# Softmax rows in step: three rows' TensorE work at one place between weight pieces

## The chip, the cores and the metric

The kernel runs on one core of a Trainium2 chip. The metric is the device time of one execution in microseconds. Five engines work side by side, each through its own queue in program order, and they are held together by semaphores: TensorE (PE in the profile, with PEld for its weight loads), VectorE (DVE), ScalarE (ACT), GpSimd (POOL) and SyncE (SP), which issues most of the DMAs.

## The reference, cut to what matters

One layer of a hybrid encoder runs on 1024 prompt frames and 64 sample frames (1088 columns in all). Of it the attention branch and the gate multiply matter here:

```
proj = rmsnorm(x) @ w_in                      # 2048 -> u, z_ssm, q, k, v, z_att, f
q, k = rmsnorm(q per head), rmsnorm(k per head)
logit[t, s] = q_t . k_s / sqrt(128) + (c_t - c_s),  s <= t
o = softmax(logit) @ v                        # 8 heads of 128
y_att = rmsnorm(o * silu(z_att)); y_ssm = ... zs * sigmoid(zs @ w_glu + b)
out = x + concat(y_ssm, y_att) @ w_out
```

A prompt row block i (128 queries) sees keys 0 to 128(i+1). The sample block (64 queries) sees 128 cached keys and its own 64.

## The kernel before, in words

The state-space stage comes first, then the attention stage, then the output projection. The attention stage is nine passes of one function, `part(h, gemm, att, ha)`, which every engine has in its own form. Pass 0 makes q, k, v and z of head 0. Passes 1 to 7 make those of head h and, between the weight matmuls, run the softmax attention of head h-1. Pass 8 (gemm False) runs the w_glu multiply with the attention of head 7 between. Every pass has 32 slots s. In each slot TensorE first multiplies one weight piece (18 matmuls, L192), and whatever the tables name for this slot follows behind it: a "place". Nine row blocks are handled in the order ROWS (0, 1, 2, 8, 3, 4, 5, 6, 7), 8 being the sample block. S_AT names the slots of the logits (L1997, L2001), T_AT those of the transposes of the probabilities (L2018, L2021), and O_AT those of the product with v (L1976, L1978).

The engines beside TensorE walk the same 32 slots in program order. In slot s ScalarE casts the high part of the weight piece s+4 (L176), which it may do once piece s is multiplied, and VectorE subtracts the low part (L180). TensorE therefore has its pieces split some three ahead. Then, if the tables say so:

- S: VectorE reduces the logits from PSUM (L1795, L1797, L1800), ScalarE takes the exponential (L1592), VectorE waits for it and multiplies by the reciprocal of the sum (L1804, L1805). The probabilities have one buffer, PR.
- T: ScalarE (L1602) and, beyond 512 columns, VectorE (L1809) copy the transposes from TB to PT.
- O: VectorE multiplies the result into ZR (L1782).
- SQ_AT (slots 8 and 19): ScalarE and VectorE square q or k (L1614, L1819, L1822: SQH, SQ and SQL). SS_AT (slots 9 and 20): TensorE sums the squares over the partitions, SQH first (L1959), then SQL (L1962), into TB.
- RT_AT, REC_AT: ScalarE takes the root; VectorE takes the reciprocals in eight pieces (L1829), for q in slots 11 to 18, for k in slots 22, 22, 23, 23, 25, 25, 26, 26. In slot 18 VectorE scales q (L1836), in slot 27 k (L1838). The squares of k wait for the scaling of q, since both use SQ.
- At slots 7, 15 and 23, where a group of eight pieces ends, ScalarE copies two thirds of the finished q, k or v out of the banks GB (L1551, L1553) and VectorE one third (L1760), as the first thing in the slot. The first piece of the next group may write bank 1 only when VectorE's copy is done. In pass 8 a group has four pieces, and ScalarE's tanh (L1544) empties all three banks at slots 3, 7, 11 and so on.

Of the kernel before, what the change touches and what calls it, by code (L numbers as in the profile page):

```python
# [21 lines left out]
D_MODEL, SEQ, DEC, PAST = 2048, 1024, 64, 128  # L22
# [5 lines left out]
P = 128  # L28
# [24 lines left out]
def build_kernel(nc, x_prompt, x_sample, cache_k, cache_v, cache_logf, state_ssm_re, state_ssm_im,  # L53
# [17 lines left out]
    def stand(eng, name):  # L71

        eng.sem_inc(sem("stand_" + name), 1)
# [46 lines left out]
    with ctx:  # L120
        sb = pool_of(ctx)
        ident = sb("ident", [P, P])
# [1037 lines left out]
        def attention(st, W, past):  # L1160
# [33 lines left out]
            NR = 9  # L1194
# [79 lines left out]


            ROWS = (0, 1, 2, 8, 3, 4, 5, 6, 7)
            S_AT = (0, 3, 5, 7, 10, 13, 16, 21, 24)
            T_AT = (2, 4, 6, 8, 12, 15, 18, 23, 26)
            O_AT = (3, 5, 7, 9, 13, 16, 19, 24, 27)
            KPT_AT = 5  # L1280
            SQ_AT = {8: (0, QR), 19: (1, KR)}
            SS_AT = {9: (0, 4), 20: (1, 7)}
            RT_AT = {9: 0, 20: 1}
            REC = 8
            REC_AT = ((11, 12, 13, 14, 15, 16, 17, 18), (22, 22, 23, 23, 25, 25, 26, 26))
# [7 lines left out]
            def keys(i):  # L1293

                return (P * (i + 1), P) if i < NR - 1 else (PAST + DEC, DEC)

            def row_at(s, at):

                return ROWS[at.index(s)], at.index(s)
# [185 lines left out]
            def scalar(act, tail):  # L1485
# [40 lines left out]
                def part(h, gemm, att, ha):  # L1526
                    last = isinstance(h, int) and h == NH - 1
                    for s in range(NPC):
# [51 lines left out]
                        if gemm and s in RT_AT:  # L1580
# [4 lines left out]
                            S.activation(SQ[:, SEQ:TOK], TB[:, 3 * 512:3 * 512 + DEC], ACT.Sqrt, bias=epsc[:],  # L1585
                                         scale=1.0 / HD).then_inc(e["rt"], 1)
                            table(ACT.Exp)
                        if att and s in S_AT:
                            i, p = row_at(s, S_AT)
                            w, n = keys(i)  # L1590
                            act.wait_ge(e["nmx"], NR * ha + p + 1)
                            S.activation(PR[0:n, 0:w], PR[0:n, 0:w], ACT.Exp, bias=nmx[0:n],  # L1592
                                         accum_out=rsum[0:n]).then_inc(e["exp"], 1)
                        if att and s == KPT_AT:
                            act.wait_ge(e["kpt_mm"], ha + 1)
                            S.copy(KPT[:], TB[:, 1024:1024 + PAST]).then_inc(e["kpt"], 1)
                        if att and s in T_AT:
                            i, p = row_at(s, T_AT)
                            act.wait_ge(e["pt_mm"], NR * ha + p + 1)
                            if i < NR - 1:  # L1600
                                b = min(i + 1, 4) * P
                                S.copy(PT[:, 0:b], TB[:, 1024:1024 + b]).then_inc(e["pt_act"], 1)  # L1602
                            else:
                                S.copy(PT[:, 0:DEC], TB[:, 1024:1024 + DEC])
                                S.copy(PT[0:DEC, P:P + DEC], TB[0:DEC, 1024 + P:1024 + P + DEC]).then_inc(e["pt_act"], 1)
                        if gemm and s in SQ_AT:
                            w, raw = SQ_AT[s]
                            act.wait_ge(e["ga"], 9 * h + 2 * w + 2)
                            act.wait_ge(e["gd"], 3 * h + w + 1)
                            if w:  # L1610
                                act.wait_ge(e["ss_mm"], 2 * h + 1)
                            elif att:
                                act.wait_ge(e["v_mm"], h)
                            S.activation(SQH[:], raw[:], ACT.Square).then_inc(e["sq"], 1)  # L1614
# [65 lines left out]
            def vector(dve, tail):  # L1680
# [66 lines left out]
                def part(h, gemm, att, ha):  # L1747
                    last = isinstance(h, int) and h == NH - 1
                    for s in range(NPC):
# [27 lines left out]
                        if att and s in O_AT:  # L1777

                            i, p = row_at(s, O_AT)
                            n = keys(i)[1]  # L1780
                            dve.wait_ge(e["o_mm"], NR * ha + p + 1)
                            V.tensor_tensor(ZR[:, i * P:i * P + n], TB[:, 4 * 512:4 * 512 + n], ZR[:, i * P:i * P + n],  # L1782
                                            ALU.mult).then_inc(e["y"], 1)
                        if att and s in S_AT:
                            i, p = row_at(s, S_AT)
                            w, n = keys(i)
                            c = 0 if i < NR - 1 else SEQ
                            if p == 0:
                                dve.wait_ge(e["in"], 48 * (ha + 1))
                            o.then(V.tensor_tensor(DM[0:n, 0:n], NCB[0:n, c + w - n:c + w], maskb[0:n, 0:n], ALU.add))  # L1790
                            dve.wait_ge(e["s_mm"], NR * ha + p + 1)
                            stand(dve, "dve")

                            if w > n:
                                V.tensor_tensor_reduce(out=PR[0:n, 0:w - n], in0=TB[0:n, 0:w - n], in1=NCB[0:n, c:c + w - n], scale=1.0,  # L1795
                                                       scalar=-3e38, op0=ALU.add, op1=ALU.max, accum_out=mx[0:n])
                            o.then(V.tensor_tensor_reduce(out=PR[0:n, w - n:w], in0=TB[0:n, w - n:w], in1=DM[0:n, 0:n], scale=1.0,  # L1797
                                                          scalar=-3e38, op0=ALU.add, op1=ALU.max, accum_out=md[0:n]))
                            if w > n:
                                V.tensor_scalar(nmx[0:n], md[0:n], mx[0:n], -1.0, ALU.max, ALU.mult).then_inc(e["nmx"], 1)  # L1800
                            else:
                                V.tensor_scalar(nmx[0:n], md[0:n], -1.0, None, ALU.mult).then_inc(e["nmx"], 1)
                            dve.wait_ge(e["exp"], NR * ha + p + 1)
                            o.then(V.reciprocal(rrec[0:n], rsum[0:n]))  # L1804
                            V.tensor_scalar(PR[0:n, 0:w], PR[0:n, 0:w], rrec[0:n], None, ALU.mult).then_inc(e["pn"], 1)  # L1805
                        if att and s in T_AT and 4 <= row_at(s, T_AT)[0] < NR - 1:
                            i, p = row_at(s, T_AT)
                            dve.wait_ge(e["pt_mm"], NR * ha + p + 1)
                            V.tensor_copy(PT[:, 512:P * (i + 1)], TB[:, 1536:1024 + P * (i + 1)]).then_inc(e["pt_dve"], 1)  # L1809
                        if gemm and s in SQ_AT:  # L1810
                            w, raw = SQ_AT[s]
                            dve.wait_ge(e["ga"], 9 * h + 2 * w + 2)
# [94 lines left out]
            def tensor(pe, tail):  # L1907
                def part(h, gemm, att, ha):
                    for s in range(NPC):
# [34 lines left out]
                        if gemm and s in SS_AT:  # L1944
# [3 lines left out]
                            pe.wait_ge(e["sq"], 2 * h + w + 1)  # L1948
                            if att:
                                pe.wait_ge(e["nmx"], NR * ha + p)  # L1950
                            if not att and w == 0:
                                pe.wait_ge(past["z_act"], 8)
                                pe.wait_ge(past["fin_ev"], 8)
                            elif not att:
                                pe.wait_ge(e["g_cum"], 2)
                                pe.wait_ge(e["g_ev"], 2)
# [7 lines left out]
                        if att and s in O_AT:  # L1964
# [12 lines left out]
                            else:  # L1977
                                T.matmul(O, CV[:], PT[:, 0:DEC], start=True, stop=False)  # L1978
                                ins = T.matmul(O, VT[0:DEC, TT - 1], PT[0:DEC, P:P + DEC], start=False, stop=True)
                            ins.then_inc(e["o_mm"], 1)  # L1980
                        if att and s in S_AT:
                            i, p = row_at(s, S_AT)
                            w, n = keys(i)
# [17 lines left out]
                                T.matmul(TB[0:DEC, 0:PAST], q, KPT[:], start=True, stop=True)  # L2001
                                ins = T.matmul(TB[0:DEC, PAST:w], q, KN[:, SEQ:TOK], start=True, stop=True)
                            ins.then_inc(e["s_mm"], 1)
                        if att and s == KPT_AT:
                            pe.wait_ge(e["in"], 48 * (ha + 1))
                            pe.wait_ge(e["pt_act"], NR * ha + sum(t < s for t in T_AT))
                            T.transpose(TB[:, 1024:1024 + PAST], CK[:], ident[:]).then_inc(e["kpt_mm"], 1)
                        if att and s in T_AT:
                            i, p = row_at(s, T_AT)
                            w, n = keys(i)  # L2010
                            pe.wait_ge(e["pn"], NR * ha + p + 1)
                            if s > KPT_AT:
                                pe.wait_ge(e["kpt"], ha + 1)
                            if p:
                                pe.wait_ge(e["pt_act"], NR * ha + p)
                            if i < NR - 1:
                                for b in range(i + 1):
                                    ins = T.transpose(TB[:, 1024 + b * P:1024 + (b + 1) * P], PR[:, b * P:(b + 1) * P], ident[:])  # L2018
                            else:
                                stand(pe, "pe")  # L2020
                                T.transpose(TB[:, 1024:1024 + DEC], PR[0:DEC, 0:PAST], ident[0:DEC, 0:DEC])  # L2021
                                ins = T.transpose(TB[0:DEC, 1024 + P:1024 + P + DEC], PR[0:DEC, PAST:w], ident[0:DEC, 0:DEC])
                            ins.then_inc(e["pt_mm"], 1)
                        if gemm and s in (KT_AT, VT_AT):
                            src, base, name = (KN, 0, "k") if s == KT_AT else (VR, 1024, "v")
                            if s == KT_AT:
# [152 lines left out]
```

## Time and profile before

| | us |
|---|---|
| median of 3 runs | 1982.18 (1981.3 to 1983.46) |
| the profiled execution | 1982.17, of which the span is 1980.6 |
| TensorE busy | 1940.0 (98%) |
| VectorE busy | 985.9 (50%) |
| ScalarE busy | 646.7 (33%) |
| GpSimd busy | 405.8 (20%) |

The mean granted clock of TensorE is 0.994 of full speed. A row of the timeline gives the start and the duration of one instruction or of a few alike. Matmuls overlap each other in the pipeline, so durations of TensorE don't add up: lengths are read there from start to start.

### The profile page before, as it was taken

What the parts mean: (1) busy time and instruction counts of PE and PEld (TensorE: products, weight loads), DVE (VectorE), ACT (ScalarE), POOL (GpSimd) and SP (SyncE); (2) the same over time, 40 slices, a digit from 0 to 9 for tenths busy, and PEclk for the clock granted to TensorE, in tenths of its full rate; (3) what the DMA queues carried; (4) which work ended last, traced back from release to release, by engine and by line L of the source; (5) the groups of instructions that cost most, each with busy time, mean ns of one, the idle gap of its engine ahead of it and who ended that gap; (6) DMA issues with size and microseconds to landing.
All of it is one profiled execution on the core that took longest, in us unless ns stands there. A gap on an engine that the chain in (4) does not pass through costs nothing.

```text
span 1980.6 us, 32524 instructions
## 1 busy us (share of the span) xinstructions
PE 1940.0 (98%) x11552; PEld 1810.3 (91%) x11552; DVE 985.9 (50%) x1899; ACT 646.7 (33%) x1274; POOL 405.8 (20%) x706
## 2 busy tenths in 40 slices
PE   5999999999999999999999999999999999999999
PEld 4899999999989999999999999999998988888887
DVE  7865566555454553645446355463565652222221
ACT  6432233332342333333433343334354441111110
POOL 5865444555210010010100101001010021010100
PEclk8999999999999999999999999999999999999999
DMA  8344343344322112121211212112165452222221
GB/s 227 105 116 103 108 111 99 107 120 122 97 55 66 36 49 70 32 86 34 72 45 34 83 34 83 37 36 82 32 234 178 139 201 91 93 94 90 96 91 46
DMA packets 194132, 180.06 MB, mean 91 GB/s; under 512 B 32179, under 2 KB 165389, under 8 KB 192853
## 3 DMA queue, kind: packets, MB, share of 16 engines
q1 hardware_dynamic: 176832, 127.97, 23.5%
q0 software_dynamic: 11712, 40.12, 6.0%
q10 hardware_dynamic: 5524, 11.14, 1.6%
q8 instruction: 38, 0.62, 0.1%
q14 instruction: 26, 0.21, 0.0%
HBM read 133.24 MB, written 45.93 MB: 90 GB/s over the span
## 4 chain that ended last, share of the span: by engine, by line
PE 90%; DVE 5%; issue 2%; DMA 1%; POOL 1%; ACT 1%; SPq 0%; DVEq 0%; POOLq 0%; ACTq 0%
PE GB L192 56%; PE TB L2087 4%; PE TB L2088 4%; PE TB L2089 4%; PE TB L1976 3%; PE TB L1997 3%; PE GB L2087 2%; PE GB L2088 2%; PE GB L2089 2%; PE TB L2018 2%; PE TB L1144 1%; PE TB L1145 1%; PE GB L1055 1%; PE TB L1134 1%; PE TB L2037 1%
## 5 line engine op out<-in xcount | busy, mean ns | idle before, releaser
L192 PE MATMUL GB<-XH,whi 128*128 128x384 f32 x2448 | 829.3, 339 | 6.0 <-DVE UP L749 5.5
L192 PE MATMUL GB<-XH,wlo 128*128 128x384 f32 x2448 | 801.5, 327 | 0.0
L192 PE MATMUL GB<-XL,whi 128*128 128x384 f32 x2448 | 798.9, 326 | 0.0
L192 PEld LDWEIGHTS GB<-XH,whi 128*128 128x128 f32 x2448 | 460.4, 188 | 21.4 <-issue 8.3
L192 PEld LDWEIGHTS GB<-XL,whi 128*128 128x128 f32 x2448 | 460.7, 188 | 5.3 <-issue 3.8
L192 PEld LDWEIGHTS GB<-XH,wlo 128*128 128x128 f32 x2448 | 459.9, 188 | 0.0
L180 DVE TENSOR_TENSOR wlo<-wraw,whi 128x256 fp32r<-128x256 f32 x412 | 206.1, 503 | 506.1 <-ACT whi L176 502.0
L176 ACT CAST whi<-wraw 128x256 fp32r<-128x256 f32 x412 | 166.4, 406 | 627.3 <-PE GB L192 618.4
L1409 POOL DMA_DIRECT2D ya_s<-ZR x7 | 4.1, 584 | 729.6 <-DVE ZR L1782 729.6
L1829 DVE RECIPROCAL SQ<-SQ 128x136 f32<-128x136 f32 x128 | 127.5, 996 | 1.1
L1592 ACT ACTIVATE PR<-PR,nmx 128x128 f32<-128x128 f32 (+8 forms) x72 | 53.4, 742 | 183.2 <-DVE nmx L1800 171.1
L2087 PE MATMUL TB<-OHI,XH 128*128 128x512 f32 x240 | 93.8, 391 | 0.0
L2088 PE MATMUL TB<-OHI,XL 128*128 128x512 f32 x240 | 93.6, 390 | 0.0
L2089 PE MATMUL TB<-OLO,XH 128*128 128x512 f32 x240 | 93.4, 389 | 0.0
L1722 DVE TENSOR_TENSOR OLO<-OLF,OHI 128x512 fp32r<-128x512 f32 x48 | 33.3, 700 | 100.6 <-ACT OHI L1524 100.6
L1882 DVE SCALAR_TENSOR_TENSOR XO<-TB,CK,XO 128x512 f32<-128x512 f32 x40 | 28.1, 747 | 109.9 <-PE TB L2089 109.9
L1976 PE MATMUL TB<-PT,VT 128*128 128x128 f32 x576 | 74.6, 275 | 0.0
L1997 PE MATMUL TB<-KN,QN 128*128 128x512 f32 (+2 forms) x192 | 72.5, 486 | 0.0
L1976 PEld LDWEIGHTS TB<-PT,VT 128*128 128x128 f32 x576 | 71.4, 191 | 0.3 <-DVE PT L1809 0.3
L1524 ACT CAST OHI<-OLF 128x512 fp32r<-128x512 f32 x48 | 29.5, 620 | 110.3 <-DMA OLF<-in_w_out 110.2
L1490 ACT ACT_TABLE_LOAD x48 | 61.6, 1283 | 0.8
L1795 DVE CUSTOM_DVE_ANT_0 PR<-TB,NCB 128x128 f32<-128x128 f32 (+3 forms) x64 | 40.9, 640 | 34.8 <-PE TB L1997 24.0
(426 smaller groups left out, 2606.3 us busy)
## 6 DMA issues: line engine op xcount, KB each, us to landing
wraw<-in_w_in SPq DMA_DIRECT2D x380, 128.0 KB, 2.2
OLF<-in_w_out SPq DMA_DIRECT2D x48, 256.0 KB, 3.0
XO<-in_x_prompt POOLq DMA_DIRECT2D x32, 256.0 KB, 4.5
out_y_prompt<-XO POOLq DMA_DIRECT2D x24, 256.0 KB, 3.4
xt<-in_x_prompt SPq DMA_DIRECT2D x5, 1024.0 KB, 5.4
NCB<-nc_s POOLq DMA_DIRECT2D x8, 608.0 KB, 5.0
us_s<-UP SPq DMA_DIRECT2D x8, 548.0 KB, 2.9
U<-us_s SPq DMA_DIRECT2D x64, 68.5 KB, 3.1
```

The source lines that it names most:

```text
L176: S.copy(whi[:, s % SPL], wraw[:, s % RAW]).then_inc(self.hi, 1)
L180: V.tensor_tensor(wlo[:, s % SPL], wraw[:, s % RAW], whi[:, s % SPL].bitcast(f32), ALU.subtract).then_inc(self.lo, 1)
L192: ins = T.matmul(group(GB if bank is None else bank, b), w[:, s % SPL, kk], x[:, k + kk, c:c + n], start=first and kk == 0 and i == 0, sto ...
L1490: o.then(S.activation(tabs[:], epsc[:], func))
L1592: S.activation(PR[0:n, 0:w], PR[0:n, 0:w], ACT.Exp, bias=nmx[0:n], accum_out=rsum[0:n]).then_inc(e["exp"], 1)
L1795: V.tensor_tensor_reduce(out=PR[0:n, 0:w - n], in0=TB[0:n, 0:w - n], in1=NCB[0:n, c:c + w - n], scale=1.0, scalar=-3e38, op0=ALU.add, op1= ...
L1829: o.then(V.reciprocal(a, a))
L1976: ins = T.matmul(O, VT[:, b], PT[:, b * P:(b + 1) * P], start=b == 0, stop=b == i)
L1997: ins = T.matmul(TB[:, c:c + cw], q, KN[:, c:c + cw], start=True, stop=True)
L2087: T.matmul(bank, YH[:, k, x], hi, start=first, stop=False)
L2088: T.matmul(bank, YL[:, k, x], hi, start=False, stop=False)
L2089: ins = T.matmul(bank, YH[:, k, x], lo, start=False, stop=last)
```

## The change

Three things are done. First, the tables put the rows in step: at most places O of one row, T of the next and S of a third stand together, in that order, so that between the S and the T of a row two to four weight pieces lie, and as many between its T and its O. Second, the blocks of code are put in that order on each engine; on ScalarE and VectorE the copy of the transposes goes ahead of the softmax. Third, the transpose of the cached keys (KPT_AT, now slot 4) goes to another bank, so that two waits on it fall away. SS_AT's second entry waits for eight rows of softmax rather than seven, and TensorE waits there for a copy of VectorE (pt_dve).

```diff
             ROWS = (0, 1, 2, 8, 3, 4, 5, 6, 7)
-            S_AT = (0, 3, 5, 7, 10, 13, 16, 21, 24)
-            T_AT = (2, 4, 6, 8, 12, 15, 18, 23, 26)
-            O_AT = (3, 5, 7, 9, 13, 16, 19, 24, 27)
-            KPT_AT = 5
+            S_AT = (0, 2, 4, 6, 10, 12, 15, 18, 22)
+            T_AT = (2, 4, 6, 10, 12, 15, 18, 22, 25)
+            O_AT = (4, 6, 10, 12, 15, 18, 22, 25, 27)
+            KPT_AT = 4
+            KPB = slice(3 * 512, 3 * 512 + PAST)
             SQ_AT = {8: (0, QR), 19: (1, KR)}
-            SS_AT = {9: (0, 4), 20: (1, 7)}
+            SS_AT = {9: (0, 4), 20: (1, 8)}
...
+                                if w:
+                                    pe.wait_ge(e["pt_dve"], 4 * ha + 2)
...
                         if att and s == KPT_AT:
                             pe.wait_ge(e["in"], 48 * (ha + 1))
-                            pe.wait_ge(e["pt_act"], NR * ha + sum(t < s for t in T_AT))
-                            T.transpose(TB[:, 1024:1024 + PAST], CK[:], ident[:]).then_inc(e["kpt_mm"], 1)
+                            T.transpose(TB[:, KPB], CK[:], ident[:]).then_inc(e["kpt_mm"], 1)
...
-                            if s > KPT_AT:
-                                pe.wait_ge(e["kpt"], ha + 1)
```

On TensorE the block of T is moved ahead of that of S, with nothing else in it changed. In the new tables the place of slot 18 holds O of row 4, T of row 5 and S of row 6, and that of slot 22 holds O of row 5, T of row 6 and S of row 7. No instruction is added or taken away.

## Rows read from the trace of the kernel before

**Rows 1.** Waits of TensorE: us in total, times, longest
```profile
PE TB L1962 <- DVE SQL L1822: 2.6, 2, 1.6
```
**Rows 2.** Timeline of TensorE, pass 5: around T of row 1
```profile
1121.24 0.31 PE L192 MATMUL GB<-XH,wlo 128*128 128x320 f32 x1
...
1122.01 0.33 PE L192 MATMUL GB<-XL,whi 128*128 128x384 f32 x1
```
**Rows 3.** Timeline, pass 5, slots 16 to 18: row blocks 4 and 5
```profile
1166.49 1.27 PE L1976 MATMUL TB<-PT,VT 128*128 128x128 f32 x10
...
1169.07 0.34 PE L192 MATMUL GB<-XL,whi 128*128 128x384 f32 x1
...
1169.25 0.82 DVE L1795 CUSTOM_DVE_ANT_0 PR<-TB,NCB 128x640 f32<-128x640 f32 x1 [0.96 <-PE TB L1997]
...
1174.83 0.82 PE L2018 MATMUL TB<-ident,PR 128*128 128x128 f32 x6
...
1175.66 0.34 PE L192 MATMUL GB<-XL,whi 128*128 128x384 f32 x1
```
**Rows 4.** Timeline, pass 5, slots 18 to 20: squares of k
```profile
1177.17 1.35 DVE L1836 SCALAR_TENSOR_TENSOR QR<-QR,qg,SQ 128x1088 f32<-128x1088 f32 x1
...
1180.25 1.29 DVE L1819 TENSOR_TENSOR SQ<-KR 128x1088 f32<-128x1088 f32 x1
1181.65 1.29 DVE L1822 TENSOR_TENSOR SQL<-SQ,SQH 128x1088 fp32r<-128x1088 f32 x1
1182.73 0.66 PE L1959 MATMUL TB<-SQH,onesr 128*128 128x512 f32 x3
1183.23 0.74 PE L1962 MATMUL TB<-SQL,onesr 128*128 128x512 f32 x3
```
**Rows 5.** Timeline of VectorE, pass 5, slot 21: softmax of row 6
```profile
1189.25 0.96 DVE L1795 CUSTOM_DVE_ANT_0 PR<-TB,NCB 128x768 f32<-128x768 f32 x1 [0.28 <-DVE DM L1790]
...
1192.68 0.42 DVE L180 TENSOR_TENSOR wlo<-wraw,whi 128x256 fp32r<-128x256 f32 x1
```
**Rows 6.** Timeline, pass 5, slot 23: copy of v, next group
```profile
1195.17 0.56 DVE L1760 COPY VR<-GB 128x384 f32<-128x384 f32 x1
...
1196.11 0.33 PE L192 MATMUL GB<-XH,whi 128*128 128x384 f32 x1
```
**Rows 7.** Timeline, pass 5, slots 24 and 25: softmax of row 7
```profile
1201.66 1.09 DVE L1795 CUSTOM_DVE_ANT_0 PR<-TB,NCB 128x896 f32<-128x896 f32 x1 [1.39 <-PE TB L1997]
1204.45 0.41 ACT L176 CAST whi<-wraw 128x256 fp32r<-128x256 f32 x1
1205.40 0.42 DVE L180 TENSOR_TENSOR wlo<-wraw,whi 128x256 fp32r<-128x256 f32 x1
1205.73 2.04 DVE L1829 RECIPROCAL SQ<-SQ 128x136 f32<-128x136 f32 x2
```
**Rows 8.** Timeline, pass 5, slot 8: squares of q
```profile
1136.43 0.31 PE L192 MATMUL GB<-XH,wlo 128*128 128x320 f32 x1
...
1138.95 1.29 DVE L1822 TENSOR_TENSOR SQL<-SQ,SQH 128x1088 fp32r<-128x1088 f32 x1
```
**Rows 9.** Timeline of ScalarE, pass 8, slots 22 and 23
```profile
1558.94 1.20 ACT L1507 ACTIVATE XH<-XL,vec 128x1088 fp32r<-128x1088 f32 x1
1560.05 1.52 ACT L1544 ACTIVATE QR<-GB,vec 128x384 f32<-128x384 f32 x3
```
**Rows 10.** Timeline of TensorE, pass 8: T of row 2
```profile
1495.93 0.55 PE L2018 MATMUL TB<-ident,PR 128*128 128x128 f32 x3 [1.92 <-DVE PR L1805]
...
1500.84 0.38 PE L1976 MATMUL TB<-PT,VT 128*128 128x128 f32 x2
```
**Rows 11.** Windows: length, busy of five engines, clock, DMA share, GB/s
```profile
1108.52:1229.69 121.17, 121.16 (x751) 116.34 (x750) 60.41 (x142) 44.04 (x93) 8.33 (x10) 1.00 0.20 55
...
1497.00:1498.00 1.00, 1.00 (x5) 1.00 (x4) 0.00 (x0) 0.00 (x0) 0.00 (x0) 0.50 1.03 332
549.00:552.00 3.00, 2.79 (x16) 2.71 (x17) 0.49 (x2) 2.94 (x4) 0.00 (x0) 1.00 0.21 49
```

More of the change, by code:

```diff
@@ L1587, in part @@
                             table(ACT.Exp)
[L1588 to L1596, printed above, removed]
                         if att and s in T_AT:
@@ L1605, in part @@
                                 S.copy(PT[0:DEC, P:P + DEC], TB[0:DEC, 1024 + P:1024 + P + DEC]).then_inc(e["pt_act"], 1)
+                        if att and s == KPT_AT:
+                            act.wait_ge(e["kpt_mm"], ha + 1)
+                            S.copy(KPT[:], TB[:, KPB]).then_inc(e["kpt"], 1)
+                        if att and s in S_AT:
+                            i, p = row_at(s, S_AT)
+                            w, n = keys(i)
+                            act.wait_ge(e["nmx"], NR * ha + p + 1)
+                            S.activation(PR[0:n, 0:w], PR[0:n, 0:w], ACT.Exp, bias=nmx[0:n],
+                                         accum_out=rsum[0:n]).then_inc(e["exp"], 1)
                         if gemm and s in SQ_AT:
@@ L1783, in part @@
                                             ALU.mult).then_inc(e["y"], 1)
+                        if att and s in T_AT and 4 <= row_at(s, T_AT)[0] < NR - 1:
+                            i, p = row_at(s, T_AT)
+                            dve.wait_ge(e["pt_mm"], NR * ha + p + 1)
+                            V.tensor_copy(PT[:, 512:P * (i + 1)], TB[:, 1536:1024 + P * (i + 1)]).then_inc(e["pt_dve"], 1)
                         if att and s in S_AT:
@@ L1805, in part @@
                             V.tensor_scalar(PR[0:n, 0:w], PR[0:n, 0:w], rrec[0:n], None, ALU.mult).then_inc(e["pn"], 1)
[L1806 to L1809, printed above, removed]
                         if gemm and s in SQ_AT:
@@ L1980, in part @@
                             ins.then_inc(e["o_mm"], 1)
+                        if att and s in T_AT:
+                            i, p = row_at(s, T_AT)
+                            w, n = keys(i)
+                            pe.wait_ge(e["pn"], NR * ha + p + 1)
+                            if p:
+                                pe.wait_ge(e["pt_act"], NR * ha + p)
+                            if i < NR - 1:
+                                for b in range(i + 1):
+                                    ins = T.transpose(TB[:, 1024 + b * P:1024 + (b + 1) * P], PR[:, b * P:(b + 1) * P], ident[:])
+                            else:
+                                stand(pe, "pe")
+                                T.transpose(TB[:, 1024:1024 + DEC], PR[0:DEC, 0:PAST], ident[0:DEC, 0:DEC])
+                                ins = T.transpose(TB[0:DEC, 1024 + P:1024 + P + DEC], PR[0:DEC, PAST:w], ident[0:DEC, 0:DEC])
+                            ins.then_inc(e["pt_mm"], 1)
+                        if att and s == KPT_AT:
+                            pe.wait_ge(e["in"], 48 * (ha + 1))
+                            T.transpose(TB[:, KPB], CK[:], ident[:]).then_inc(e["kpt_mm"], 1)
                         if att and s in S_AT:
@@ L2003, in part @@
                             ins.then_inc(e["s_mm"], 1)
-                        if att and s == KPT_AT:
-                            pe.wait_ge(e["in"], 48 * (ha + 1))
-                            pe.wait_ge(e["pt_act"], NR * ha + sum(t < s for t in T_AT))
-                            T.transpose(TB[:, 1024:1024 + PAST], CK[:], ident[:]).then_inc(e["kpt_mm"], 1)
[L2008 to L2011, printed above, removed]
-                            if s > KPT_AT:
-                                pe.wait_ge(e["kpt"], ha + 1)
[L2014 to L2023, printed above, removed]
                         if gemm and s in (KT_AT, VT_AT):
```

## The prediction, made before the changed kernel was seen

> **What bounds the kernel.** I read the page first: TensorE is busy for 1940.0 of 1980.6 us, and the chain that ended last is 90% TensorE. So an engine beside it costs nothing until it makes TensorE wait. Next the waits of TensorE: it hardly has any in the attention passes [rows 1], so there is little to win and the question is what can be lost. Last the timeline of one pass, slot by slot. I do all arithmetic on pass 5; it takes 121.17 us [rows 11], and the tables treat passes 1 to 7 alike. All lengths are from start to start. A weight matmul follows another after 0.17 us (after a narrow one 0.15), so a place is as long as from its first start to the second weight start behind it, less 0.17. The place of slot 16 is 1169.07 - 0.17 - 1166.49 = 2.41, and from its end (1168.90) to the T at 1174.83 two pieces take 5.93, one 2.97 [rows 3]. The T there takes 1175.66 - 0.17 - 1174.83 = 0.66 for six blocks, 0.11 each, and the place of slot 16 holds five key blocks of O and six of S, 2.41 / 11 = 0.22 each, twice a T block: nothing is left over for the turn from weights to attention and back, so gathering places saves nothing by itself. I take 0; a gain of 0.05 a turn would be the most that these roundings can hide, with nine places fewer in each of 8 passes 3.6 us.
>
> **What the change takes away.** T of row 1 in slot 4 is one piece behind its S. It should begin at 1121.24 + 0.15 = 1121.39 and end 0.22 later; the weight matmuls resume at 1122.01 - 0.17 = 1121.84, so 0.23 us is a wait for VectorE [rows 2]. With two pieces between it is gone, in eight passes: 1.8. In pass 8 T of row 2 comes after 1.9 us of idle time. Behind this one the piece is slow: from 1495.93 to 1500.84 there are three transposes (0.33) and one piece (2.97), and the remaining 1.6 us is the clock [rows 10], granted at 0.50, which is 1.2 GHz, after full speed before the idle [rows 11]. Row 2's softmax there waits behind VectorE's gate of w_glu, and will still be some 0.5 late. The row's lateness is an estimate between 0 and 1.9. Pass 8 gains 1.9 + 1.6 - 0.5 = 3.0 with it. The transpose of the cached keys in another bank moves 0.1 us of work and loosens waits that nobody is seen to feel: 0.
>
> **What it adds, first place: slot 18.** Here S of row 6 now stands on VectorE ahead of the last reciprocal of q, of the scaling of q and, in slot 19, of the squares of k, which TensorE wants in slot 20. Before, slot 18 had no S. Put the beginning of the place at 0. VectorE's reduce began 1169.25 - 1166.49 = 2.76 after the place of slot 16, which had O of row 4 and S of row 5 [rows 3]; with one key block more (0.22) and the T of row 5 (0.66) it is 3.64, and the place ends 0.35 earlier, at 3.29. VectorE then needs 3.43 for row 6's softmax, its wait for ScalarE included [rows 5], 1.02 for a reciprocal (half of 2.04 [rows 7]), 1.35 for scaling q, 0.35 for the split of a weight piece (as from 1205.40 to 1205.73 [rows 7]), 1.40 from SQ to SQL and 1.29 for SQL [rows 4]: 3.64 + 3.43 + 1.02 + 1.35 + 0.35 + 1.40 + 1.29 = 12.48. TensorE gets to SQH at 3.29 + 5.93 = 9.22 and to SQL 0.50 later [rows 4], 9.72. It waits 2.76, call it 2.8 with the semaphore, in each of seven passes. The new wait for pt_dve is met long before.
>
> **Second place: slot 22.** S of row 7 and then two reciprocals of k stand on VectorE ahead of its copy of v in slot 23, and the first piece of z in slot 24 may not write bank 1 before that copy. Before, S of row 6 stood in 21; the copy ended at 1195.73 and bank 1 was begun at 1196.11 [rows 6], 0.38 to spare. Now O of row 5, T of row 6 and S of row 7 make the place: against slot 16 one block more of O (0.22), two more of S (0.44) and seven of T (0.77), so the reduce of row 7 begins at 2.76 + 1.43 = 4.19, and the place ends at 3.84. Softmax of row 7 takes 1205.40 - 1201.66 = 3.74, two reciprocals 2.1 [rows 7], the copy 0.56 [rows 6]: done at 10.59, seen at 10.64. TensorE wants bank 1 at 3.84 + 2.97 and bank 0's share of a piece, six matmuls of 384 columns out of 6528 columns in all, 2.97 x 0.353 = 1.05: 7.86. It waits 2.8, seven times. ScalarE's copies come at about 7.0 to 7.5 and lie within this wait.
>
> **Third: slot 8.** The sample row's T leaves slot 8, and with it the cover of VectorE's squares of q. The piece ended at 1136.58 and SQL at 1140.24, 3.66 later [rows 8]; TensorE will want it at 2.97 + 0.50 = 3.47. With 0.05 for the semaphore, 0.25 each, 1.7 in seven. In pass 0, where no attention covers these slots, exactly this wait is on record, 1.6 and 1.0 [rows 1]; that is the upper bound.
>
> **Pass 8** has no squares, but ScalarE's tanh stands behind the exponential. In slot 22 ScalarE is free 1204.45 - 1201.66 = 2.79 after the reduce begins [rows 7], at 6.99, then needs 1.11 for a split and 0.58 for a third of the tanh [rows 9], 8.7 against bank 0 wanted at 6.81: 1.9. Slot 18 gives 0.5 in the same way. Together 2.4, against the gain of 3.0.
>
> Elsewhere each softmax gets more time than before, and the split weights are still some three pieces ahead: VectorE's worst lag of 10 us in slot 22 delays the split of piece 27, wanted only four pieces, two places and the wait later, some 20 us after that place began. No DMA is moved; GpSimd's copies wait for the O of slot 27, which stays.
>
> **The clock.** How much a wait costs beyond itself has one precedent each way: 1.92 us idle was followed by half clock for one piece (1.6 us lost) [rows 10, 11], 1.6 us and less was not [rows 1, 11]. The fourteen new waits of 2.8 are nearer to the first. Bounds are 0 and 14; I take ten, since one row is thin evidence: 16. The Trainium skill (TensorE: Matmul & The Clock Gate, section HAM oscillation) tells of a kernel in which the wait at every tile sent the engine back to its lower clock, so that the price was paid again each time. By that all fourteen would pay; no run before shows a repeated wait.
>
> **Sum.** Per pass 1 to 7: 2.8 + 2.8 + 0.25 = 5.85, times 7 is 41.0. T of row 1: -1.8. Pass 8: 2.4 - 3.0 = -0.6. Clock: 16. In all 54.6. The profiled execution has 1982.17 and the median 1982.18, so 2036 (rounded down for the turns that may be saved).
>
> **Rivals.**
> (a) All fourteen waits bring the low clock: 14 x 1.6 = 22 instead of 16, 2042, and up to 2046 with 0.38 more per pass for slot 8 and pass 8's wait. None does: 2020, which is 16 less. These are sizes of the same mechanism; chance 0.20 for the first, 0.10 for the second.
> (b) Only one of the two places binds, because VectorE comes to slot 18 or 22 with its softmax faster than in before's chain, or TensorE's own delay in slot 20 carries the rest. Then 7 x 2.8 and some five slow pieces go: 2036 - 20 - 8 = 2008. Against it: both sums rest on VectorE's strict order and miss their time by 2.8 of some 10. Chance 0.10.
> (c) Faster: the spread works as cover and nothing new is late. That needs VectorE to come 2.8 us earlier in both slots, for instance if the reduce and the scaling overlap the wait for ScalarE with the next work, which the program order denies. Price: 1.8 and 3.0 less, 1977. It decides from the point where both sums fall under 9.7 and 7.9. Chance 0.08.
> (d) The change does nothing visible, its waits gained and lost cancelling within 4 us: 0.02.
> (e) Something more is late than I found, such as a split, which ends each time in a longer wait: beyond 2046, 0.08.
>
> **Numbers.** The main case (some clocks fall) has 0.42, and 2030 to 2041. With (a) and (b) the range 2000 to 2046 holds 0.82. Faster or slower by 0.2% (4 us) is about what a measurement of this kernel can tell: faster 0.08, same 0.02, slower 0.90.
>
> **What would show it.** In the changed profile, waits of TensorE should list L1962 for SQL with about 20 us over seven times 2.8, and L192 for VectorE's L1760 with about 20 over seven. L2018's wait for PR should shrink to under 1. The passes should be 127 to 130 us long instead of 121.2, and windows behind slots 20 and 24 should show a clock under 1.00. If passes 1 to 7 stay at 121, the two sums are wrong; if they are near 124, one of them is.

## The result and the profile after

| | before | changed |
|---|---|---|
| median, us | 1982.82 (1981.3 to 1984.39, 4 runs) | 2048.72 (2031.4 to 2055.04, 4 runs) |
| profiled execution, us | 1982.17, span 1980.6 | 2031.4, span 2029.8 |
| TensorE busy | 98% | 96% |
| ratio to before | | 1.032 (95% interval 1.028 to 1.037) |

The kernel became 3.2% slower. The direction was as forecast, and the time is 2.7 us above the end of the stated range. The profiled execution is the fastest of the four, and the spread of the runs, 24 us against 3 before, is itself part of the finding. Four more executions of the same kernel, under "The changed kernel once more", have a median of 2038.43, and all eight one of 2041.3. The ratios given here and below leave out two executions in a slow state, one of the kernel before (6823 us) and one of "Only the early rows moved" (4244 us).

The page of the changed kernel, its head, then the first line on TensorE in the costliest groups (the idle time before it and what ended it stand at the right):

```profile
PE 1953.8 (96%) x11552; PEld 1820.0 (90%) x11552; DVE 987.2 (49%) x1899; ACT 647.6 (32%) x1274; POOL 407.6 (20%) x706
...
L192 PE MATMUL GB<-XH,whi 128*128 128x384 f32 x2448 | 830.2, 339 | 24.6 <-DVE VR L1761 13.4
```

Every engine has as many instructions as before. The busy time of the engines beside TensorE is the same within 2 us. TensorE's grew by 13.8 us, since a matmul lasts longer at half clock and the profile models its end, and its idle time grew from 40.6 to 76.0 us. The waits of TensorE in the changed kernel (who waited for whom, us in total, times, longest) answer [rows 1]:

```profile
PE TB L1965 <- DVE SQL L1823: 21.8, 15, 2.6
PE GB L192 <- DVE VR L1761: 13.4, 7, 1.9
...
PE GB L192 <- ACT VR L1552: 3.4, 7, 0.5
PE GB L192 <- ACT QR L1545: 2.2, 2, 1.8
```

L1965 is the sum of squares (L1962 before), L1761 VectorE's copy of v (L1760 before). Both waits were to be looked for. The second shows 13.4 us where about 20 were named; ScalarE's 3.4 belong to the same place, as the rows of slot 24 below show. The wait for the probabilities, up to 1.9 us in [rows 10], is not in this list, but it is 1.4 us in the second trace of the same kernel; see "Both moves" for what it hangs on.

The timeline of pass 3, slots 18 to 20, VectorE and TensorE, answers [rows 4]:

```profile
951.84 0.96 DVE L1800 CUSTOM_DVE_ANT_0 PR<-TB,NCB 128x768 f32<-128x768 f32 x1 [1.04 <-PE TB L2017]
...
955.27 1.00 DVE L1830 RECIPROCAL SQ<-SQ 128x136 f32<-128x136 f32 x1
956.30 1.35 DVE L1837 SCALAR_TENSOR_TENSOR QR<-QR,qg,SQ 128x1088 f32<-128x1088 f32 x1
957.28 0.57 PEld L1962 LDWEIGHTS TB<-SQH,onesr 128*128 128x128 f32 x3
957.43 0.65 PE L1962 MATMUL TB<-SQH,onesr 128*128 128x512 f32 x3
957.57 0.42 DVE L180 TENSOR_TENSOR wlo<-wraw,whi 128x256 fp32r<-128x256 f32 x1
957.91 1.28 DVE L1820 TENSOR_TENSOR SQ<-KR 128x1088 f32<-128x1088 f32 x1
...
959.30 1.29 DVE L1823 TENSOR_TENSOR SQL<-SQ,SQH 128x1088 fp32r<-128x1088 f32 x1
...
960.65 0.75 PE L1965 MATMUL TB<-SQL,onesr 128*128 128x512 f32 x3 [2.57 <-DVE SQL L1823]
```

Read it from top to bottom: the softmax of row 6 fills VectorE up to 955.27, the last reciprocal and the scaling of q stand behind it, and SQ and SQL behind those. TensorE is at the sum at 957.43, before VectorE has begun SQ. From L1962 to L1965 there are 3.22 us where there were 0.50 [rows 4]: 2.7 us of wait.

The same pass, slots 22 to 24, answers [rows 6, 7]:

```profile
971.46 1.09 DVE L1800 CUSTOM_DVE_ANT_0 PR<-TB,NCB 128x896 f32<-128x896 f32 x1 [1.12 <-PE TB L2017]
...
974.71 0.45 PE L192 MATMUL GB<-XH,whi 128*128 128x384 f32 x1 [0.49 <-ACT VR L1552]
...
975.20 2.03 DVE L1830 RECIPROCAL SQ<-SQ 128x136 f32<-128x136 f32 x2
977.35 0.56 DVE L1761 COPY VR<-GB 128x384 f32<-128x384 f32 x1
...
977.96 0.45 PE L192 MATMUL GB<-XH,whi 128*128 128x384 f32 x1 [1.93 <-DVE VR L1761]
```

The copy of v, which had 0.38 us to spare before, ends at 977.91. TensorE stops first 0.49 us at bank 0 for ScalarE, whose copy is behind the exponential of row 7, and then 1.93 us at bank 1 for VectorE. The profile counts an idle stretch only from the modelled end of the last matmul. From start to start three pieces after this place take 11.86 us here against 3 x 2.97 = 8.91, so the place costs 2.95.

Windows of the changed kernel (length, busy of PE, PEld, DVE, ACT and POOL, granted clock, DMA share and rate) over passes 3 and 5 and over two stretches of pass 5 answer [rows 11]:

```profile
882.79:1009.94 127.15, 122.00 (x751) 116.61 (x750) 60.42 (x142) 44.14 (x93) 8.71 (x11) 1.00 0.19 52
1137.05:1268.47 131.42, 126.27 (x752) 120.87 (x751) 60.42 (x142) 44.15 (x93) 8.32 (x10) 0.96 0.19 50
...
1217.00:1219.00 2.00, 2.00 (x8) 2.00 (x7) 0.00 (x0) 1.51 (x3) 0.00 (x0) 0.50 0.03 9
...
1236.00:1239.00 3.00, 3.00 (x12) 3.00 (x11) 0.43 (x1) 0.40 (x1) 0.00 (x0) 0.50 0.00 0
```

Pass 3 has the waits and full clock: 127.15 against 121.17, 6.0 us more. Pass 5 has the same waits and is 4.3 us longer still. Behind the wait of slot 20 and behind that of slot 24 the clock stands at half. The difference is 1.5 us behind the first (two pieces in 7.48 instead of 5.95) and 2.7 behind the second (three pieces in 14.59 instead of 11.86). Of the 14 places of this kind in the trace (two in each of passes 1 to 7) four have half clock behind them, 7.3 us together.

The clock also falls at a place that the change doesn't touch. In pass 0 TensorE waits twice, the second time 2.3 us after the first, as it did before:

```profile
546.90 0.73 PE L1962 MATMUL TB<-SQH,onesr 128*128 128x512 f32 x3 [1.04 <-issue]
549.20 0.75 PE L1965 MATMUL TB<-SQL,onesr 128*128 128x512 f32 x3 [1.57 <-DVE SQL L1823]
...
551.00:553.00 2.00, 2.00 (x7) 2.00 (x7) 0.00 (x0) 1.95 (x4) 0.00 (x0) 0.50 0.11 32
```

In [rows 11] the window behind these waits had full clock. Of the ten traces in this case six have half clock there (this one, and those of five of the eight experiments, the old slots under the new order among them), and TensorE is 1.3 to 2.6 us later by it. So the prediction's reading that 1.6 us and less leave the clock alone holds for the trace that it was taken from and not in general.

### The profile page after: what moved, and what is told of

It is laid out like the page before. It is cut to its first block, busy times and chain, and to the rows that moved or that the text cites. A ratio compares the mean times of both kernels' runs of the same rounds, so it can differ in the third digit from the quotient of the medians.

```text
span 2029.8 us, 32480 instructions
## 1 busy us (share of the span) xinstructions
PE 1953.8 (96%) x11552; PEld 1820.0 (90%) x11552; DVE 987.2 (49%) x1899; ACT 647.6 (32%) x1274; POOL 407.6 (20%) x706
## 4 chain that ended last, share of the span: by engine, by line
PE 85%; DVE 8%; issue 4%; POOL 1%; ACT 1%; DMA 0%; SPq 0%; DVEq 0%; ACTq 0%; POOLq 0%
PE GB L192 53%; PE TB L2087 4%; PE TB L2088 4%; PE TB L2089 4%; PE TB L1979 3%; PE TB L2017 3%; PE GB L2087 2%; PE GB L2089 2%; PE GB L2088 2%; PE TB L1992 2%; DVE SQ L1830 1%; DVE SQL L1823 1%; DVE SQ L1820 1%; PE TB L2037 1%; PE TB L1144 1%
## 5 line engine op out<-in xcount | busy, mean ns | idle before, releaser
L192 PE MATMUL GB<-XH,whi 128*128 128x384 f32 x2448 | 830.2, 339 | 24.6 <-DVE VR L1761 13.4
```

The lines of the kernel that those rows point to most:

```text
L192: ins = T.matmul(group(GB if bank is None else bank, b), w[:, s % SPL, kk], x[:, k + kk, c:c + n], start=first and kk == 0 and i == 0, sto ...
```

## Experiments

Theory: the new slots of rows 6 and 7 put a softmax on VectorE ahead of work that TensorE wants soon, 2.75 us in slot 20 and 2.95 in slot 24 of seven passes, and behind such waits the clock falls. Rivals: the order of the code on the engines, the new bank or the wait for pt_dve costs the time; and for the clock, the long places of slower matmuls bring it down, not the waits.

### Old slots under the new order

```diff
-            S_AT = (0, 2, 4, 6, 10, 12, 15, 18, 22)
-            T_AT = (2, 4, 6, 10, 12, 15, 18, 22, 25)
-            O_AT = (4, 6, 10, 12, 15, 18, 22, 25, 27)
-            KPT_AT = 4
+            S_AT = (0, 3, 5, 7, 10, 13, 16, 21, 24)
+            T_AT = (2, 4, 6, 8, 12, 15, 18, 23, 26)
+            O_AT = (3, 5, 7, 9, 13, 16, 19, 24, 27)
+            KPT_AT = 5
...
-            SS_AT = {9: (0, 4), 20: (1, 8)}
+            SS_AT = {9: (0, 4), 20: (1, 7)}
```

> The changed kernel with the four slot tables of before put back (S_AT, T_AT, O_AT, KPT_AT and the 7 of SS_AT); the new order of the code blocks, the new bank of the cached keys and the new wait for pt_dve stay. My theory, that the slots of rows 6 and 7 put VectorE's work for k and v behind a softmax: the time of before, 1982 to 1984, and TensorE waits less than 3 us for SQL in all. Rival, that the order on ScalarE and VectorE (copy of the transposes ahead of the softmax), the bank or the wait for pt_dve costs the time: clearly above 1990.

Measured: 1981.46 us against 1982.14, ratio 0.9999 (0.9989 to 1.0008). TensorE waits 2.6 us for SQL in all, both times in pass 0, as before. To within 0.1% (2 us) the new order, the bank and the new wait cost nothing and bring nothing. What the change does to the time beyond that is in the tables.

### Scaling of q one slot earlier

```diff
-            REC_AT = ((11, 12, 13, 14, 15, 16, 17, 18), (22, 22, 23, 23, 25, 25, 26, 26))
-            QN_AT, KN_AT, YSQ_AT, KT_AT, VT_AT = 18, 27, 29, 29, 31
+            REC_AT = ((11, 12, 13, 13, 14, 14, 16, 17), (22, 22, 23, 23, 25, 25, 26, 26))
+            QN_AT, KN_AT, YSQ_AT, KT_AT, VT_AT = 17, 27, 29, 29, 31
```

> The changed kernel with one thing moved: VectorE takes the last reciprocals of q two to a slot in 13 and 14, and scales q in slot 17 instead of 18. My theory: SQL in slot 20 is ready at 3.64 + 3.43 + 0.35 + 1.40 + 1.29 + 0.05 = 10.16 after the place of slot 18 began, against 9.72 wanted, so the wait falls from 2.75 to 0.4 in each of 7 passes; 16 us are saved at full clock, and the wait at L1761 stays as it is, 13 us. In all 2006 at full clock, and up to 15 more where the seven waits left bring the low clock. Rival, that the wait for SQL hangs on something else, the place's own length or ScalarE's square: it stays over 2 us and the time over 2020.

Measured: 2019.22 us (2018.3 to 2020.63), ratio 1.019 (1.017 to 1.020). Slot 20 of pass 3, VectorE and TensorE:

```profile
950.53 0.42 DVE L180 TENSOR_TENSOR wlo<-wraw,whi 128x256 fp32r<-128x256 f32 x1
950.87 1.29 DVE L1820 TENSOR_TENSOR SQ<-KR 128x1088 f32<-128x1088 f32 x1
952.27 1.29 DVE L1823 TENSOR_TENSOR SQL<-SQ,SQH 128x1088 fp32r<-128x1088 f32 x1
...
952.69 0.65 PE L1962 MATMUL TB<-SQH,onesr 128*128 128x512 f32 x3
953.62 0.76 PE L1965 MATMUL TB<-SQL,onesr 128*128 128x512 f32 x3 [0.27 <-DVE SQL L1823]
```

The squares now follow the softmax of row 6 directly, and L1962 to L1965 is 0.93 us, so 0.43 of wait are left, as computed. The wait at L1761 is untouched, 13.4 us in 7. The time lies near the upper end of what was expected (2006 to 2021). The trace shows why: behind the wait of slot 24 the clock is at half in all seven passes, and each time the three pieces take 1.5 us longer. This is the window in pass 3:

```profile
972.00:974.00 2.00, 2.00 (x9) 2.00 (x8) 1.14 (x2) 0.00 (x0) 0.00 (x0) 0.50 0.26 66
```


### First reciprocals of k one slot later

```diff
-            REC_AT = ((11, 12, 13, 14, 15, 16, 17, 18), (22, 22, 23, 23, 25, 25, 26, 26))
+            REC_AT = ((11, 12, 13, 14, 15, 16, 17, 18), (23, 23, 24, 24, 25, 25, 26, 26))
```

> The changed kernel with one thing moved: VectorE's first two reciprocals of k leave slot 22, so that all eight stand in slots 23, 23, 24, 24, 25, 25, 26, 26, behind the copy of v. My theory: the copy ends at 4.19 + 3.74 + 0.56 + 0.05 = 8.54 after the place of slot 22 began, against 7.86 wanted, so TensorE loses 0.7 there instead of 2.8 in each of 7 passes, of which 0.5 is its wait for ScalarE at bank 0; 15 us are saved at full clock. In all 2008 at full clock, and up to 15 more by the clock behind the waits for SQL, which stay at 2.6. Rival, that the reduce of row 7 or the place itself holds bank 1: the time stays over 2020.

Measured: 2019.71 us (2016.06 to 2020.18), ratio 1.018 (1.017 to 1.020). The wait at L1761 has left the list of waits; ScalarE's at bank 0 and the one for SQL stay:

```profile
PE TB L1965 <- DVE SQL L1823: 21.8, 15, 2.6
...
PE GB L192 <- ACT VR L1552: 3.4, 7, 0.5
```

Behind the wait of slot 20 the clock is at half in six of the seven passes, at 1.4 to 1.6 us each; pass 1 keeps full clock. So each of the two places holds about half of the loss, and neither hides the other.

### Both moves

The two edits above together.

> Both moves together on the changed kernel: reciprocals and scaling of q one slot earlier, the first reciprocals of k one slot later. My theory: what is left per pass is 0.45 for SQL in slot 20, 0.7 at bank 1 in slot 24 and 0.35 in slot 9, so against the changed kernel at full clock (2022.6) 16.3 and 15 us less: 1991 to 1994, and no half clock behind waits under 1 us, so a granted clock of 0.994 to 0.997. Rival, that the two waits hide one another or a third wait (the new place of slot 22 on ScalarE, k ready late for slot 29) takes their place: over 2000.

Measured: 1993.17 us (1990.08 to 1995.8), ratio 1.006 (1.004 to 1.007), granted clock 0.996 to 0.998. With both causes gone the kernel is 56 us faster than the first four executions of the changed one, and the single moves save 29 each; against the median of all eight it is 48, and 22 each. That the two add up is better seen in the waits, which the clock doesn't blur: this kernel has 2.3 us less in slot 20 and 2.15 less in slot 24 of a pass, as the single moves have, and it is 30 us faster than the kernel with half of the filling below, which has nearly full clock throughout. What is left against before is a wait of 0.45, 0.8 and 0.35 in slots 20, 24 and 9. These slots are now gathered as the change gathers them, and TensorE gains nothing from it. There is also a wait of 1.9 us for the probabilities again, once, at the T of row 2 in pass 8. Row 2's softmax stands on VectorE behind the gate of w_glu (L1688), and the gate waits for a transfer (KO from zs_s). First the gate in the first trace of the changed kernel, then gate and T in this one:

```profile
1536.96 1.29 DVE L1688 SCALAR_TENSOR_TENSOR QR<-QR,VR 128x1088 f32<-128x1088 f32 x1 [2.90 <-DMA KO<-zs_s]
...
1502.87 1.29 DVE L1688 SCALAR_TENSOR_TENSOR QR<-QR,VR 128x1088 f32<-128x1088 f32 x1 [5.28 <-DMA KO<-zs_s]
...
1508.78 0.55 PE L1992 MATMUL TB<-ident,PR 128*128 128x128 f32 x3 [1.86 <-DVE PR L1810]
```

Eight traces have this row in its new slots. Where VectorE waits 2.9 and 3.1 us for the transfer, T is on time; where it waits 3.9, 4.2, 4.2, 4.6, 4.8 and 5.3, T is late by 0.5, 0.8, 0.8, 1.2, 1.4 and 1.9. The 4.8 with 1.4 are the second trace of the changed kernel. So whether T is late hangs on when a transfer lands; why that differs was not looked into.

### The waits filled with idle work

Ahead of the wait for bank 1 in slot 24, and ahead of that for SQL in slot 20 (w is 1 for k):

```diff
+                                    if att and s == 24:
+                                        for _ in range(10):
+                                            T.matmul(TB[:, 4 * 512 + 128:4 * 512 + 512], onesr[:], XH[:, 0, 0:384], start=True, stop=True)
                                     pe.wait_ge(e["gd"], 3 * h + s // 8)
...
+                            if att and w:
+                                for _ in range(14):
+                                    T.matmul(TB[:, 4 * 512 + 128:4 * 512 + 512], onesr[:], XH[:, 0, 0:384], start=True, stop=True)
                             pe.wait_ge(e["sql"], 2 * h + w + 1)
```

> The changed kernel with the two long waits filled: in passes 1 to 7 TensorE does 14 matmuls of 384 columns (2.4 us) ahead of its wait for SQL in slot 20, and 10 (1.7 us) ahead of its wait for bank 1 in slot 24, into a part of a bank that nobody reads. They are extra work inside time that was idle. My theory of the clock, that what lies between the runs of the changed kernel (2031 to 2055) is only how many of the 14 waits are followed by half clock: the time comes to 2021 to 2025 in every execution, the granted clock to 0.994 as before, and the spread of the runs shrinks below 3 us. Rival, that the clock falls for another reason (long places of slower matmuls and transposes): no change in clock or spread. Second rival, that the waits cost only themselves: the same time as the changed kernel or more.

Measured: 2024.84 us (2022.35 to 2028.41), ratio 1.021 (1.019 to 1.023), granted clock 0.994 to 0.997. TensorE does 168 matmuls more than the changed kernel and finishes 24 us earlier than the median of its first four executions, 16 earlier than that of all eight. The spread is 6 us, not under 3. Slot 20 of pass 3 on TensorE:

```profile
956.01 0.65 PE L1965 MATMUL TB<-SQH,onesr 128*128 128x512 f32 x3
956.50 2.68 PE L1968 MATMUL TB<-XH,onesr 128*128 128x384 f32 x14
959.24 0.76 PE L1971 MATMUL TB<-SQL,onesr 128*128 128x512 f32 x3
```

The sum over SQL comes 3.23 us after that over SQH, as in the changed kernel (3.22): the work lies wholly inside the wait. The places and their order are those of the changed kernel, so it is the idle time that lets the clock fall, not the kind of work.

### Half of the filling

Seven and five matmuls instead of 14 and 10.

> The changed kernel with only half of the fill: 7 matmuls ahead of the wait for SQL, 5 ahead of that for bank 1, so that idle stretches of 1.4 to 1.6 us and of 1.0 us are left. My theory of the clock: waits of 1.6 us and less were followed by full clock in before, so the time is that of the filled kernel, 2022 to 2026, with a clock of 0.994 or more. Rival, that any idle time in these slots brings the low clock in proportion: half of what the changed kernel loses, 2035 to 2040.

Measured: 2023.36 us (2021.7 to 2026.66), ratio 1.022 (1.020 to 1.023), granted clock 0.993 to 0.997. The waits that are left:

```profile
PE TB L1971 <- DVE SQL L1823: 12.7, 15, 1.6
...
PE GB L192 <- DVE VR L1761: 7.3, 7, 1.1
```

The longest of the first, 1.6, is that of pass 0; in slot 20 of passes 1 to 7 about 1.3 us of idle time are left. Slot 20 of pass 3 on TensorE shows it:

```profile
954.75 1.47 PE L1968 MATMUL TB<-XH,onesr 128*128 128x384 f32 x7
957.49 0.76 PE L1971 MATMUL TB<-SQL,onesr 128*128 128x512 f32 x3 [1.27 <-DVE SQL L1823]
```

None of the seven brings the lower clock: the two pieces behind them take 5.95 to 5.97 us each time. In both filled kernels the clock is full throughout passes 1 to 7 and at half behind the two waits of pass 0. So 2023 to 2025 is the changed kernel at very nearly full clock: the waits alone cost 42 us. In the first four executions (66 us over before) the clock cost the other 24, in the median of all eight 17.

### The changed kernel once more

> The changed kernel itself once more, for a second trace and more runs. My theory: every pass has the same waits (2.6 for SQL, 0.5 and 1.9 at the banks of slot 24) and the runs differ only by how many of them are followed by half clock and for how long: between 2023 (none) and 2055, time and granted clock on one line, about 1980 us x the clock's shortfall. The first trace showed half clock behind 4 of the 14, three costing 1.5 us and one 2.7; a slower execution must show more of them, or longer ones. Rival: another part of the program (state-space stage, pass 8, output projection) differs between the runs.

Measured: 2038.43 us (2037.25 to 2044.65), ratio 1.030 (1.028 to 1.031), clock 0.985 to 0.989. The windows behind one wait of slot 24 (pass 6) and one of slot 20 (pass 7):

```profile
1364.00:1368.00 4.00, 4.00 (x14) 4.00 (x15) 2.03 (x3) 0.24 (x1) 0.00 (x0) 0.50 0.13 33
...
1476.00:1480.00 4.00, 3.58 (x11) 3.39 (x12) 0.70 (x2) 2.19 (x3) 0.00 (x0) 0.50 0.13 33
```

Here nine of the 14 places have half clock behind them: seven cost 1.3 to 1.6 us, two 2.8, 16.0 together (the stretches of both traces after the same place are compared with those at full clock, 5.95 and 11.86). The waits themselves are the same as in the first trace, 21.8, 13.4 and 3.4 us. Over all eight runs of the changed kernel time and clock go together: 2031.4 at 0.990, 2037 and 2038 at 0.989, 2039 at 0.986, 2043 and 2045 at 0.983 and 0.985, 2054 and 2055 at 0.979. The executions of 2054 and 2055 us lose 31 against the filled kernels, 2.2 for each of the 14 places. No trace of one of these was taken, so how those 31 are spread over the places stays open. An estimate: pass 5 of the first trace lost 4.3 to the clock (1.5 and 2.7), and seven such passes would make 30.

### Only the early rows moved

The edit is shown against the tables before; the new order of the code, the new bank and the wait for pt_dve are in this kernel too, which by themselves brought nothing (the old slots under the new order).

```diff
-            S_AT = (0, 3, 5, 7, 10, 13, 16, 21, 24)
+            S_AT = (0, 2, 4, 7, 10, 13, 16, 21, 24)
             T_AT = (2, 4, 6, 8, 12, 15, 18, 23, 26)
             O_AT = (3, 5, 7, 9, 13, 16, 19, 24, 27)
-            KPT_AT = 5
+            KPT_AT = 4
```

> The old slots for rows 8 and 3 to 7, and the new ones for the logits of rows 1 and 2 alone: S_AT = (0, 2, 4, 7, 10, 13, 16, 21, 24), T_AT and O_AT as before, the cached keys in their new bank in slot 4. Nothing is put ahead of VectorE's work for q, k and v. My theory: T of row 1 no longer waits (8 x 0.23), and in pass 8 the late T of row 2 (1.9) with the slow piece behind it (1.6) shrinks to 0.5: 1977 to 1979, faster than before by 0.15 to 0.25%. Rival, that row 2's softmax in pass 8 is as late as before, since it stands behind the gate either way: 1980 to 1981, not to be told from before.

Measured: 1977.94 us against 1981.66, ratio 0.998 (0.997 to 0.999). It is faster than both kernels, though little: 3.7 us against before, with ten executions at 1975.9 to 1980.0 and fourteen of before at 1980.2 to 1983.1. The T of row 2 in pass 8, with what is before and behind it:

```profile
1494.86 0.31 PE L192 MATMUL GB<-XH,wlo 128*128 128x320 f32 x1
1495.01 0.54 PE L1992 MATMUL TB<-ident,PR 128*128 128x128 f32 x3
1495.31 0.42 PE L192 MATMUL GB<-XH,whi 128*128 128x384 f32 x1
```

The window around it has full clock, where the one in [rows 11] had half:

```profile
1490.00:1500.00 10.00, 10.00 (x67) 9.72 (x66) 6.03 (x18) 4.67 (x10) 0.58 (x1) 1.00 0.82 280
```

The T follows the weights after 0.15 us, where it came after 1.92 us of idle time in [rows 10]. This is the good part of the change, and it needs two entries of one table. It has little to spare: VectorE waited 3.1 us for its transfer in this trace, and in others of the same slots, where it waited longer, T was late ("Both moves").

## Why the prediction was right and wrong

**Right: where and why.** Slot 20 waits 2.72 to 2.75 us for SQL, computed 2.76. Slot 24 loses 2.95, computed 2.8; of it 0.5 is ScalarE's at bank 0, which the prediction laid inside VectorE's. Slot 9 loses 0.35 (1.50 against 1.15 for the two sums together), computed 0.25. The place of slot 22 is 3.83 long, computed 3.84. The waits of slots 20 and 24 are shown by taking them away: moving the two pieces of VectorE's work left waits of 0.43 and 0.8, computed 0.44 and 0.7. That gathering places saves nothing is shown by the kernel with both moves, which is gathered and has no gain.

**Right: what goes away.** T of row 1 no longer waits, and pass 8 loses its late T of row 2 together with the slow piece. The kernel with early rows alone shows the worth of these: 3.7 us, where 5.3 were counted less 0.5. The remaining lateness of row 2, an estimate of 0.5, was 0 in the first trace of the changed kernel and 1.4 in the second. It follows the transfer that the gate waits for, which the prediction didn't have in view. Of pass 8's new waits for the tanh, 1.9 and 0.5 were computed, and ScalarE's L1545 shows 1.8 and 0.4.

**Wrong: the clock's term.** The sum was 38.6 us of waits and 16 of clock. Measured are 42 of waits (the kernels with filled waits) and, in the median of the first four runs, 24 of clock. The waits are 3 us over the sum. Of these 0.15 and 0.1 per pass are the sizes of slots 24 and 9, together 1.8. Another 1.3 is spread over the passes: pass 3 is 5.98 longer, while its three waits less the one that fell away make 5.8. The rest is within what pass 0's clock does from one execution to the next. The clock is the larger error: one fall was priced at 1.6 us from the single case in the trace, and all 14 at 22, which set the end of the range at 2046. In the traces a fall cost 1.3 to 2.8, and in the executions of 2054 us it must be 2.2 on average over all 14. A price read from one row was used as if it had no spread, and the range followed it. With 14 x 2.8, a price known only since, as the upper bound the range would have reached 2059 and held every run.

How far the number was off is in part the draw. The second four executions of the same kernel have a median of 2038.43, 2 us from the 2036 of the sum, and 17 us of clock in the median of all eight is close to the 16. The forecast had no term for executions of one kernel differing by 24 us, and that they would was not foreseen.

**Right by half: how often.** Ten falls of 14 were taken. The traces show four and nine, in executions of 2031 and 2039 us; with one place left they show seven of seven and six of seven. The times of the slowest executions suggest that nearly all fall there, but no trace shows it. The limit behind the count was not right either: "1.6 us and less was not" followed by half clock is what one trace of the kernel before shows, and behind the waits of 1.04 and 1.57 us in pass 0 six of ten traces have half clock.

The Trainium skill (TensorE: Matmul & The Clock Gate, section HAM oscillation) tells of a kernel that paid the price of the fall again at every one of its waits. The traces agree only in part: 4 and 9 of 14 in the changed kernel, 7 of 7 and 6 of 7 in those with one place left. By it the case of all 14 would have been the likeliest, which at 1.6 each is 2042, still below the first median.

The other rivals fell. A single binding place is ruled out, since each move alone took away its own wait and left the other as it was; a gain by cover, and no visible change, by the result. The first median lies beyond 2046, where rival (e) put it, but not for its reason: no further wait came in.

## What to carry to other kernels

When a long chain (here a softmax of 3.4 to 3.7 us on VectorE) is moved, list what else its in-order queue owes to the bounding engine in the next slots, and compute when each is due: the piece that suffers is not the one that is moved. A wait on TensorE of some 2 us, or two shorter ones close together, is to be priced twice, for itself and for the clock behind it, and the second with a spread. A threshold read from one trace is a guess. Before slots are redrawn for a whole table, move only the entries that a wait in the profile points to: here two of them brought the gain of 3.7 us, and the new slots of rows 6 and 7 nearly all of the loss.

## What the runs showed of the hardware

TensorE's clock stood at one of two levels, 2.4 or 1.2 GHz, and what idle time did to it was not the same from one execution to the next. A wait of 1.3 us, and one of 0.5 with one of 1.1 close behind, left it at 2.4 GHz in all seven passes of the half-filled kernel, and a single one of 1.8 us for the tanh in pass 8 did so in all seven traces that have it. A wait of 1.9 us for row 2 in pass 8 was followed by 1.2 GHz in the trace of before and not in that of the kernel with both moves. In pass 0 two waits of 1.04 and 1.57 us, with 0.7 us of work between them, were followed by 1.2 GHz in six of ten traces.

The waits of slots 20 and 24 (2.6 us, and 0.5 and 1.9 close together), in a changed kernel whose passes are alike instruction for instruction, were followed by 1.2 GHz in four of 14 places in one execution and nine in another. With one of the two places left it was seven of seven and six of seven. What decides it stays open. One fall cost 1.3 to 1.6 us or, in three of the 26, 2.7 to 2.8. So identical waits made eight executions of one kernel differ by 24 us. With 168 useless matmuls put into the waits, or 84, the eight executions of the two filled kernels lie within 7 us, 16 to 18 below the median of the changed kernel's eight.
